# The order of split products within a weight panel: three per tile, or three passes over the whole panel

## The reference

```python
u = rmsnorm(h, norm_mix); u_ssm, q, k, v = split(u @ w_in)
y_ssm, y_attn = s5_branch(u_ssm, ...), stick_breaking_attention(q, k, v)
h = h + (g_ssm * (y_ssm @ w_up_ssm) + g_attn * (y_attn @ w_up_attn)) @ w_out
h = rmsnorm(h + relu(rmsnorm(h, norm_mlp) @ w_ff1) ** 2 @ w_ff2, norm_final)
for l in range(2):                                     # hybrid_layer
    u = h * (1 + scale) + shift                        # from silu(c) @ w_ada
    proj = u @ w_in_2[l]                               # a_in, a_gate, b_in, b_gate, latents, ...
    y_a, y_b, y_c = conv 31 branch, conv 3 branch, latent attention branch
    h = layer_norm(ALPHA * h + gate * ((g_a*y_a + g_b*y_b + g_c*y_c) @ w_o))
```

## Time and profile before

| | |
|---|---|
| median of 3 runs | 1085.34 us (1080.2 to 1085.47) |
| the profiled execution: its own time | 1085.24 us |
| its span, first to last instruction | 1083.5 us |
| TensorE busy | 1019.8 us, 94% |
| weight loads busy | 963.2 us, 89% |
| VectorE, ScalarE, GpSimd busy | 690.2, 552.3, 367.9 us |
| mean granted TensorE clock | 0.975 |
| bytes read from HBM | 177.26 MB, 165 GB/s |

### The profile page before, as it was taken

The page is one execution under the profiler, slowest core; times in us unless marked ns, Lnnn a source line. Parts: engine busy times, 40 slices in busy tenths (PEclk is TensorE's granted clock), DMA queues, the critical chain, the costliest instruction groups (busy, mean ns, idle before and its releaser), DMA issues.

```text
span 1083.5 us, 19478 instructions
## 1 busy us (share of the span) xinstructions
PE 1019.8 (94%) x8072; PEld 963.2 (89%) x8072; DVE 690.2 (64%) x1041; ACT 552.3 (51%) x642; POOL 367.9 (34%) x151
## 2 busy tenths in 40 slices
PE   5989999899999999978999999999889999999995
PEld 4977777789999999968999999999689999899994
DVE  4859898673425222446867886855557778877553
ACT  4455666545544344356554645543664546446532
POOL 3079881003887878300065430000000556300000
PEclk8999999999999999989999999999898999999998
DMA  8644444666855664463644445553636343564601
GB/s 273 195 157 141 148 149 161 200 213 197 271 181 170 194 191 161 131 207 128 196 130 143 156 156 188 168 190 117 189 122 227 124 155 128 171 193 153 210 5 39
DMA packets 159495, 179.56 MB, mean 166 GB/s; under 512 B 5040, under 2 KB 141744, under 8 KB 159408
## 3 DMA queue, kind: packets, MB, share of 16 engines
q1 hardware_dynamic: 159024, 177.22, 50.8%
q0 software_dynamic: 384, 1.10, 0.3%
HBM read 177.26 MB, written 1.05 MB: 165 GB/s over the span
## 4 chain that ended last, share of the span: by engine, by line
PE 77%; DVE 7%; issue 7%; ACT 4%; DMA 3%; POOL 2%; SPq 0%; ACTq 0%; DVEq 0%; POOLq 0%
PE pg L1737 22%; PE pg L1739 22%; PE pg L1738 22%; PE p_s L1833 2%; ACT w_hi L904 2%; PE p_y L1899 1%; PE p_o L1923 1%; DVE w_lo L1212 1%; PE p_s L1731 1%; DVE rows L1263 1%; DMA raw<-in_w_ff 1%; ACT area L879 1%; DVE area L1221 1%; PE pg L1777 1%; DVE va_lo L1221 1%
## 5 line engine op out<-in xcount | busy, mean ns | idle before, releaser
L1737 PE MATMUL pg<-u_hi,w_hi 128*128 128x256 f32 x1536 | 447.8, 292 | 27.1 <-DVE u_lo L1221 15.8
L1738 PE MATMUL pg<-u_lo,w_hi 128*128 128x256 f32 x1536 | 439.8, 286 | 0.0
L1739 PE MATMUL pg<-u_hi,w_lo 128*128 128x256 f32 x1536 | 439.4, 286 | 0.0
L803 POOL TENSOR_TENSOR w_lo<-raw,w_hi 128x2048 fp32r<-128x2048 f32 x61 | 284.8, 4678 | 322.9 <-ACT w_hi L904 322.9
L1737 PEld LDWEIGHTS pg<-u_hi,w_hi 128*128 128x128 f32 x1536 | 300.1, 195 | 35.6 <-DVE w_lo L1212 17.9
L904 ACT ACTIVATE w_hi<-raw 128x2048 fp32r<-128x2048 f32 (+3 forms) x153 | 275.0, 1803 | 73.7 <-issue 31.3
L1738 PEld LDWEIGHTS pg<-u_lo,w_hi 128*128 128x128 f32 x1536 | 300.3, 196 | 0.7
L1739 PEld LDWEIGHTS pg<-u_hi,w_lo 128*128 128x128 f32 x1536 | 300.0, 195 | 0.0
L1212 DVE TENSOR_TENSOR w_lo<-raw,w_hi 128x2048 fp32r<-128x2048 f32 (+2 forms) x92 | 190.6, 2084 | 62.7 <-ACT w_hi L904 62.6
L910 ACT ACTIVATE area<-pg 128x512 f32<-128x512 f32 (+1 forms) x92 | 54.1, 588 | 152.6 <-PE pg L1739 140.4
L1737 PE MATMUL pg<-vb_hi,w_hi 128*128 128x256 f32 x320 | 91.2, 285 | 5.5 <-DVE area L1239 3.1
(11 more groups left out here) (212 smaller groups left out, 1456.7 us busy)
## 6 DMA issues: line engine op xcount, KB each, us to landing
raw<-in_w_in SPq DMA_DIRECT2D x68, 1024.0 KB, 5.2
raw<-in_w_ff SPq DMA_DIRECT2D x32, 1024.0 KB, 5.7
raw<-in_w_ada SPq DMA_DIRECT2D x24, 1024.0 KB, 5.2
raw<-in_w_gate SPq DMA_DIRECT2D x8, 1024.0 KB, 7.7
raw<-in_w_o SPq DMA_DIRECT2D x8, 1024.0 KB, 5.3
raw<-in_w_out SPq DMA_DIRECT2D x4, 1024.0 KB, 8.6
raw<-in_w_b_out SPq DMA_DIRECT2D x4, 1024.0 KB, 5.1
raw<-in_w_c_out SPq DMA_DIRECT2D x4, 1024.0 KB, 5.0
```

The costliest lines, as they stand in the source:

```text
L803: pool.tensor_tensor(w_lo[:, s, 0:n], raw[:, r, 0:n], w_hi[:, s, 0:n].bitcast(F32), ALU.subtract).then_inc(sem(f"raw_free{r}"), 1)
L1737: pe.matmul(dst, w_h, x_h, start=first, stop=False)
L1738: pe.matmul(dst, w_h, x_l, start=False, stop=False)
L1739: return pe.matmul(dst, w_l, x_h, start=False, stop=last_)
```

## The change

Within a panel the loop over products becomes the outer one. All `w_hi*x_hi` of the panel come first, then all `w_hi*x_lo`, then all `w_lo*x_hi`. TensorE waits for `w_hi` and the pieces of `hi` in the first pass, for `lo` in the second, and for `w_lo` (`slot_free`) ahead of the third. In panels of two groups each pass goes over both groups, so both banks are filled at the same time; ukv does this with its groups in pairs. ff2 now waits for its two pieces one by one. Panels v, ada and the v part of ukv keep their loops, and no other engine's program changes.

```diff
-            def blocks(q, g, widths, x_hi, x_lo, waits):
+            def blocks(q, banks, hi_ready, lo_ready, x_hi, x_lo):
                 wh, wl = slot(w_hi, q), slot(w_lo, q)
-                group_start(g)
-                turns = [(i, k) for i in range(len(widths)) for k in range(q["kt"])]
-                mixed = len(waits) > 1
-                if mixed:
-                    turns.sort(key=lambda at: at[1])
-                for i, k in turns:
-                    a, m = widths[i]
-                    if i == 0 and k in waits:
-                        pe.wait_ge(*waits[k])
-                    ins = three(...)
-                ins.then_inc(sem("groups"), 1)
+                def one_pass(g, widths, w, x, ready):
+                    turns = [(i, k) for i in range(len(widths)) for k in range(q["kt"])]
+                    if len(hi_ready) > 1:
+                        turns.sort(key=lambda at: at[1])
+                    for i, k in turns:
+                        a, m = widths[i]
+                        if i == 0 and k in ready:
+                            pe.wait_ge(*ready[k])
+                        ins = pe.matmul(pg[g % 2][0:m, i * T:i * T + T], w[:, k, a:a + m], x[:, k, :],
+                                        start=x is x_hi and w is wh and (i, k) == turns[0], stop=w is wl and (i, k) == turns[-1])
+                    return ins
+                for n, (g, widths) in enumerate(banks):
+                    group_start(g)
+                    one_pass(g, widths, wh, x_hi, {} if n else hi_ready)
+                for n, (g, widths) in enumerate(banks):
+                    one_pass(g, widths, wh, x_lo, {} if n else lo_ready)
+                pe.wait_ge(*slot_free(q))
+                for g, widths in banks:
+                    one_pass(g, widths, wl, x_hi, {}).then_inc(sem("groups"), 1)
...
-                pe.wait_ge(*slot_free(q))
-                waits = {}
+                if job == "v":
+                    pe.wait_ge(*slot_free(q))
+                else:
+                    pe.wait_ge(sem("w_hi"), over("w_hi", q["s"]))
+                highs, lows = {}, {}
                 if job == "ff2":
-                    pe.wait_ge(sem("ff_lo"), over("ff_lo", 2 * ch + 1))
+                    highs = {2 * i: (sem("ff_hi"), over("ff_hi", 2 * ch + i)) for i in range(2)}
+                    lows = {2 * i: (sem("ff_lo"), over("ff_lo", 2 * ch + i)) for i in range(2)}
...
-                    waits = {a: (sem("lo"), over("lo", key, j)) for j, (a, b) in enumerate(o["pieces"])} if key not in begun else {}
+                    if key not in begun:
+                        highs = {a: (sem("hi"), over("hi", key, j)) for j, (a, b) in enumerate(o["pieces"])}
+                        lows = {a: (sem("lo"), over("lo", key, j)) for j, (a, b) in enumerate(o["pieces"])}
```

More of the change, by code:

```diff
@@ L1733, in sum_tiles @@
                 return ins
[L1735 to L1739, removed]
             def group_start(g):
@@ L1746, in _ @@
             begun = set()
-            def blocks(q, g, widths, x_hi, x_lo, waits):
+            def blocks(q, banks, hi_ready, lo_ready, x_hi, x_lo):
                 wh, wl = slot(w_hi, q), slot(w_lo, q)
-                group_start(g)
-                turns = [(i, k) for i in range(len(widths)) for k in range(q["kt"])]
-                mixed = len(waits) > 1
-                if mixed:
-                    turns.sort(key=lambda at: at[1])
-                for i, k in turns:
-                    a, m = widths[i]
-                    if i == 0 and k in waits:
-                        pe.wait_ge(*waits[k])
-                    ins = three(pg[g % 2][0:m, i * T:i * T + T], wh[:, k, a:a + m], wl[:, k, a:a + m],
-                                x_hi[:, k, :], x_lo[:, k, :], k == 0 and not (mixed and i),
-                                (i, k) == turns[-1] if mixed else k == q["kt"] - 1)
-                ins.then_inc(sem("groups"), 1)
+                def one_pass(g, widths, w, x, ready):
[17 more added lines that the diff above has]
+                    one_pass(g, widths, wl, x_hi, {}).then_inc(sem("groups"), 1)
             def panel(p, _):
@@ L1806, in panel @@
                 elif job == "uq":
-                    for i in range(2):
-                        blocks(q, g + i, [(P * (2 * i + j), P) for j in range(2)], xh, xl, waits if i == 0 else {})
+                    blocks(q, [(g + i, [(P * (2 * i + j), P) for j in range(2)]) for i in range(2)], highs, lows, xh, xl)
                 elif job == "ukv":
-                    for i in range(4):
-                        blocks(q, g + i, [(P * (2 * i + j), P) for j in range(2)], xh, xl, waits if i == 0 else {})
+                    for n in range(0, 4, 2):
+                        blocks(q, [(g + i, [(P * (2 * i + j), P) for j in range(2)]) for i in (n, n + 1)],
+                               {} if n else highs, {} if n else lows, xh, xl)
                     wh, wl = (slot(x, q).rearrange("p k (h m) -> p k h m", h=HEADS)[:, :, :, NOPE:P] for x in (w_hi, w_lo))
@@ L1822, in panel @@
                 else:
+                    banks = []
                     for i in range(q["groups"]):
                         left = min(256, (P if job == "k_rope" else q["cols"]) - 256 * i)
-                        blocks(q, g + i, [(256 * i + P * j, min(P, left - P * j)) for j in range((left + P - 1) // P)],
-                               xh, xl, waits if i == 0 else {})
+                        banks.append((g + i, [(256 * i + P * j, min(P, left - P * j)) for j in range((left + P - 1) // P)]))
+                    blocks(q, banks, highs, lows, xh, xl)
             def sum_piece(key, src, j, region):
```

## The result

The changed kernel takes 1093.2 us (median of 7 runs, 1090.21 to 1096.56), the kernel before 1083.65 us (7 runs). The ratio is 1.009, with a 95% interval of 1.0065 to 1.0116: slower by 9 to 10 us. The profiled execution took 1093.79 us with a span of 1092.1 us, 8.6 us more than the span before.

The account below looks back on a forecast made before the run. TensorE, busy for 94% of the span, was taken to bound the kernel, leaving only its gaps to win. The terms sum to +8.95 us on 1085.24, giving 1094.2, stated as 1094, with a range of 1084 to 1103.

Parts of the forecast that it names:

- w_lo not awaited at the start: At a1 and kv_lat, both layers: waits for w_lo shrink or go, -8.9 and -3.0 us.
- Both banks at branch1: At branch1 the second bank is needed after 8 matmuls, not 24; +8.4 us for both layers, half speed included.
- Four pieces, three passes: Panels fed in four pieces finish later: u +3.2 and +3.5 us by layer, u2 +1.0, w_o +3.7 for both layers.
- the rule of 36 matmuls left behind the last piece: In pieced panels, 36 matmuls remain after the last hi piece, 4.3 us at full speed, where 12 remained before.
- w_o: At the w_o panel: +1.35 us, and +0.5 for an even chance of half speed; +3.7 for both layers.
- First block: up_attn and up_ssm start earlier, -5.45 us; panel out gives back +1.85, and +0.9 for half speed; together -2.7.
- Hand-overs: Banks emptied slightly late: ff2 and branches +0.7 us, uq and ukv +2.8, sums behind ff2 +0.75.
- Behind the last panel: After the last panel: no change predicted, 0 us.
- the clock stays up: Rival: gaps of 3.7 us and pieces 2 us apart leave the granted clock full; 1084 us, chance 0.2.
- Hand-overs are late everywhere: Rival: each of 39 two-bank panels loses 0.3 us more, 12 in all; 1106 us, chance 0.13.
- Nothing moves: Rival: other waits at once fill those that go, and pieces and banks cost little; 1085 us, chance 0.05.
- only the gains: Rival: no +8.4 us at branch1 and no +11.4 for the pieces; 1074 us, chance 0.07.

Follow-up runs that it names:

- e10: Changed kernel with one bank at a time in the sixteen ff2 panels alone; 1092.97 us, ratio 1.0079 to the kernel before.
- e2: Changed kernel with the old order and old waits in the panels whose operand arrives in four pieces; 1082.03 us, ratio 0.9994 to the kernel before.
- e1: Changed kernel, but two-group panels finish their first bank before beginning the second; 1079.46 us, ratio 0.9977 to the kernel before.
- e5: Changed kernel with 28 extra unused matmuls filling the gap before branch1's second bank, both layers; 1088.23 us, ratio 1.0058 to the kernel before.
- e6: Changed kernel with one bank at a time in branch1's two panels of each layer only; 1087.35 us, ratio 1.0043 to the kernel before.
- e8: Changed kernel with VectorE's take of the last panel before branch1 moved ahead of a conv_a step; 1090.79 us, ratio 1.0065 to the kernel before.
- e3: Changed kernel with both edits, one bank at a time and the old order in the pieced panels; 1069.1 us, ratio 0.9878 to the kernel before.
- e7: e3 with VectorE's take of the last panel before branch1 moved ahead of a conv_a step; 1073.63 us, ratio 0.9905 to the kernel before.
- e11: e3, but each piece of two tiles in pieced panels runs its w_hi*x_hi matmuls first; 1065.26 us, ratio 0.9832 to the kernel before.
- e12: e11 with the take before branch1 ahead of conv_a and the second conv_a step behind branch1; 1061.38 us, ratio 0.9816 to the kernel before.

## Why the prediction was right

It said 1094 and the median is 1093.2, of the same sign and by the mechanism named. By its own steps:

- *w_lo not awaited at the start*: -8.9 and -3.0 predicted, -8.65 and -3.5 measured. What was late next, the bank, was read rightly from the earlier trace rows.
- *Both banks at branch1*: +8.4 predicted, +7.7 measured. 1.9 was right in both layers; the clock cost 2.6 and 1.3 where I took 2.3 twice, and e10 shows that either layer can draw either price.
- *Four pieces, three passes*: the rule of 36 matmuls left behind the last piece was right, and e2 takes its cost back at all of these panels. Layer 0 was over-estimated, +1.3 for +3.2. From the last u_hi to the panel's last matmul it went from 3.3 to 5.7 us, near the forecast. But TensorE came to the panel 1.1 us later than before, and the pieces did not: they stand behind w_hi, which waits for its weights to land, at 463.30 before and 463.25 after. So 1.1 us of the costs ahead of it were absorbed. I had not asked what else sets the start of the pieces. ScalarE's w_hi ahead of the pieces, before and then after, and TensorE at this panel after:

```profile
463.30 1.06 ACT L904 ACTIVATE w_hi<-raw 128x1024 fp32r<-128x1024 f32 x1 [3.73 <-DMA raw<-in_w_in]
```

```profile
463.25 1.06 ACT L904 ACTIVATE w_hi<-raw 128x1024 fp32r<-128x1024 f32 x1 [2.55 <-DMA raw<-in_w_in]
```

```profile
466.46 1.20 PE L1754 MATMUL pg<-u_hi,w_hi 128*128 128x256 f32 x4 [4.65 <-ACT u_hi L879]
...
472.33 1.22 PE L1754 MATMUL pg<-u_hi,w_hi 128*128 128x256 f32 x4 [0.76 <-ACT u_hi L879]
473.35 3.03 PE L1754 MATMUL pg<-u_lo,w_hi 128*128 128x256 f32 x16
476.22 1.96 PE L1754 MATMUL pg<-u_hi,w_lo 128*128 128x256 f32 x15
```

- *w_o*: +1.35 was exact in layer 0; in layer 1 it was 1.6 beside the clock. The even chance of half clock came out once: layer 1 has it (1049.0 to 1052.4), layer 0 not. The five kernels e1, e5, e6, e8 and e10 have the same panel without it and are 1.5 us shorter there.
- *First block*: -2.7 predicted, -1.6 measured. The gains of 5.3 are there. I expected the give-back at out; it came one panel sooner, at the bank of up_ssm's second panel, with half clock behind it (222.9 to 226.4). VectorE's take and TensorE there, after:

```profile
220.76 0.68 DVE L1239 TENSOR_TENSOR area<-pg,area 128x512 f32<-128x512 f32 x1
...
221.59 1.19 PE L1754 MATMUL pg<-va_hi,w_hi 128*128 128x256 f32 x8 [1.94 <-DVE area L1239]
```

- *Hand-overs*: the term that was too small. +0.5 and +0.75 predicted for ff, 2.2 measured; uq and ukv 3.7 for 2.8; the branches 0.9 for 0.2. I compared a take of 0.20 + 0.69 us with 8 matmuls of 0.96 less 0.02 and called it nearly covered; at each hand-over it costs about 0.1 more than that. Why, no experiment shows.
- *Behind the last panel*: nothing predicted, -1.6 measured. That is the clock's chance: after the same gap the same 16 matmuls of the last sums run at half speed in the execution before and at full speed in the one after, 1.7 us apart. Before, then after:

```profile
1067.12 5.41 PE L1833 MATMUL p_s<-area,ones 128*128 128x256 f32 x16 [1.91 <-ACT area L879]
```

```profile
1077.36 3.72 PE L1841 MATMUL p_s<-area,ones 128*128 128x256 f32 x16 [1.90 <-ACT area L879]
```

Three readings in the prediction do not hold, though the sum does not hang on them. That every stretch at half speed follows a gap of about 2 us or more is true of the rows it shows, not of the whole trace: the stretch from 87.6 to 91.0 before stands behind gaps of 0.86 and 1.11 us, and the one at w_o of layer 1 after behind 0.53 and 0.97. At a1 the gap left is 3.18 - 2.35 = 0.83 us, not 0.95; 0.84 was measured. And the terms of "the clock stays up" add to -1.75, so 1083.5 and not 1084.

Of the rivals, "the clock stays up" is refuted by the 0.50 behind branch1 and by e5. "Hand-overs are late everywhere" had a real core, but some 0.14 us per ff2 panel (2.2 / 16), not 0.3. "Nothing moves" and "only the gains" did not happen. Yet e3 shows that the gains were to be had without most of the costs: 1069 us against my 1074 for that rival.

Luck has a part in the number. The first block, the hand-overs and w_o came out 4.4 us dearer than predicted; u in layer 0 (1.9), branch1 (0.7), kv_lat (0.5), u in layer 1 (0.3) and the chance of 1.6 at the end made up for it. The sum is better than its terms.

## What to carry over

Waiting later and ordering differently are two edits, even when one loop makes both. Here the order cost 35 us, and the later waits won 25 within it; with the costly order taken out (e3) the waits still won 14 against the kernel before. To put a product late so that its operand may come late, do it within what arrives together (a piece, a bank), not across it: TensorE then stands idle before the last arrival and has more left behind it. At w_o of layer 0, 36 matmuls were left for 12, and the panel ended 1.35 us later. And when the second of two buffers is wanted after 8 matmuls in place of 24, look for the one place where its release stands behind other work; branch1 cost more than any other kind of panel.

## What was not expected of the hardware

VectorE's w_lo took 6.71 us beside GpSimd's, not 2.28, when it began 0.15 after it; in e7 6.72. Where GpSimd began second, its own took 5.6 in place of 4.6.

The clock does not answer equally to equal gaps. In ff2 the same wait of 1.95 us stands in e3 and, with 1.94, in e11. In one it is followed by half clock, in the other not. In e3, the matmul behind the gap and the window after it:

```profile
337.72 1.39 PE L1754 MATMUL pg<-vb_hi,w_hi 128*128 128x256 f32 x8 [1.95 <-issue]
```

```profile
338.50:341.90 3.40, 3.40 (x19) 3.40 (x18) 0.00 (x0) 0.00 (x0) 3.40 (x2) 0.50 0.68 262
```

The same in e11:

```profile
338.53 1.19 PE L1754 MATMUL pg<-vb_hi,w_hi 128*128 128x256 f32 x8 [1.94 <-issue]
```

```profile
339.50:342.90 3.40, 3.40 (x30) 3.40 (x30) 0.69 (x1) 0.00 (x0) 3.40 (x2) 1.00 0.61 237
```

In 3.4 us 19 matmuls run, or 30; the ledger has 1.5 us between the two there. Nor is 1.95 us a bound: e12 has a gap of 1.77 at 228.78 with half clock behind it, and e3 one of 1.78 at 226.71 without. The cost of such a gap is some 1.3 to 1.5 us (11 matmuls less, by 0.12; the ledger's step), or nothing. That this makes part of the spread between executions of one kernel is likely, but only one execution of each was profiled.
